# A routed mixture-of-experts layer: each row's expert choices renumbered by the block that serves them, half of them loaded during the last round, shared expert and routing tables interleaved anew

## The reference

```python
def moe_ffn(h, lp):
    x2 = h.reshape(bsz * t, d)
    scores = jax.nn.sigmoid((x2 @ lp['w_router']).astype(F32))          # 64 experts
    choice = scores + lp['b_router'].astype(F32)
    ...                                                                  # 4 of 8 expert groups
    _, idx = lax.top_k(jnp.where(expert_mask, choice, -jnp.inf), TOP_K)  # 8 choices of a row
    gate = jnp.take_along_axis(scores, idx, axis=1)
    gate = gate / jnp.sum(gate, axis=-1, keepdims=True) * ROUTE_SCALE
    routed = routed_experts(x2, idx, gate.astype(x2.dtype), lp['w_exp_gate'], lp['w_exp_up'], lp['w_exp_down'])
    shared = swiglu(x2, lp['w_sh_gate'], lp['w_sh_up'], lp['w_sh_down'])
    return (routed + shared).reshape(bsz, t, d)
# swiglu(x, wg, wu, wd) = (silu(x @ wg) * (x @ wu)) @ wd, inner width 256
# layer: x1 = x + g1 * mix(...);  y = x1 + g2 * moe_ffn(rms_norm(x1) * (1 + sc2) + sh2)
```

## Time and profile before

| | |
|---|---|
| median of 3 runs | 1614.6 us (1612.56 to 1618.46) |
| profiled execution | 1618.61 us, its span 1616.7 us |
| mean granted TensorE clock | 0.967 |
| TensorE, VectorE, ScalarE, POOL busy | 93%, 41%, 22%, 31% of the span |
| first weight transfer issued; first gate-up | 895.1 us; 935.1 us |
| last down product ends; last scatter issued | 1554.1 us; 1557.7 us |

### The profile page before, as it was taken

One profiled execution on the slowest core, in us unless ns is written; L12 is line 12 of the kernel. 1 busy time (PEld: TensorE's weight loads), 2 busy tenths in 40 slices (PEclk: granted clock), 3 DMA queues, 4 the chain that ended last, 5 costly groups with the idle time before them and its releaser, 6 DMA issues.

```text
span 1616.7 us, 21285 instructions
## 1 busy us (share of the span) xinstructions
PE 1510.2 (93%) x8196; PEld 819.0 (51%) x8196; DVE 655.4 (41%) x1119; ACT 357.6 (22%) x674; POOL 499.7 (31%) x545
## 2 busy tenths in 40 slices
PE   4999998999999979999999899999999998999977
PEld 3444455777688758888445533333333333333323
DVE  4799981232322566447466511111111111111147
ACT  3111133422533323331223111111111111111120
POOL 3121101211000014000000356665666665666510
PEclk9999999999999889999899989999999999999979
DMA  9787644778322657648111799999899899979668
GB/s 311 267 325 286 235 161 159 273 281 291 127 79 72 198 187 271 200 161 315 64 67 40 293 403 417 409 413 395 319 364 412 325 420 398 362 273 411 241 261 335
DMA packets 138630, 437.30 MB, mean 270 GB/s; under 512 B 31574, under 2 KB 59594, under 8 KB 103726
## 3 DMA queue, kind: packets, MB, share of 16 engines
q0 software_dynamic: 65088, 303.29, 48.6%
q1 hardware_dynamic: 68128, 122.39, 21.9%
q10 hardware_dynamic: 5344, 10.65, 1.7%
HBM read 507.52 MB, written 45.61 MB: 342 GB/s over the span
## 4 chain that ended last, share of the span: by engine, by line
PE 81%; DMA 8%; DVE 3%; issue 3%; ACT 2%; POOL 1%; another core or an unknown queue 1%; SPq 0%; POOLq 0%; ACTq 0%; DVEq 0%
PE bank L2440 18%; PE bank L2078 14%; PE bank L1989 12%; PE bank L2465 9%; PE bank L2309 4%; DMA arena<-in_w_exp_up_dram,arena 4%; PE bank L2297 4%; PE bank L2426 3%; PE bank L2111 2%; DMA arena<-expert_rows 2%; PE bank L2513 1%; DMA arena<-in_w_in_dram 1%; PE bank L2096 1%; POOL arena L721 1%; PE bank L2236 1%
## 5 line engine op out<-in xcount | busy, mean ns | idle before, releaser
L2440 PE MATMUL bank<-arena 128*64 128x512 f32 x1536 | 348.5, 605 | 10.7 <-DMA arena<-in_w_exp_up_dram,arena 6.2
L2078 PE MATMUL bank<-arena 128*128 128x260 f32 x1024 | 237.5, 387 | 0.0
L2440 PEld LDWEIGHTS bank<-arena 128*64 128x64 f32 x1536 | 108.3, 137 | 215.1 <-issue 209.4
L2078 PEld LDWEIGHTS bank<-arena 128*128 128x128 f32 x1024 | 191.9, 192 | 33.8 <-ACT arena L951 2.7
L1989 PE MATMUL bank<-arena 128*128 128x512 f32 (+1 forms) x448 | 189.8, 579 | 0.0
L2465 PE MATMUL bank<-arena 128*64 128x512 f32 x768 | 183.9, 603 | 5.5 <-issue 4.3
L1824 DVE TENSOR_TENSOR arena<-arena,bank 128x256 f32<-128x256 f32 x48 | 20.3, 423 | 362.0 <-ACT arena L1150 218.0
L1989 PEld LDWEIGHTS bank<-arena 128*128 128x128 f32 x448 | 83.5, 189 | 97.9 <-issue 90.5
L721 POOL DMA_INDIRECT arena<-in_w_exp_gate_dram,arena x96 | 96.0, 1000 | 72.7 <-issue 60.4
L721 POOL DMA_INDIRECT arena<-in_w_exp_down_dram,arena x96 | 96.2, 1002 | 29.8 <-issue 28.7
L721 POOL DMA_INDIRECT arena<-in_w_exp_up_dram,arena x96 | 96.1, 1001 | 29.3 <-issue 29.3
(11 more groups left out here) (454 smaller groups left out, 1790.6 us busy)
## 6 DMA issues: line engine op xcount, KB each, us to landing
arena<-in_w_ada_dram SPq DMA_DIRECT2D x24, 1024.0 KB, 7.6
arena<-in_w_merge_gate_dram SPq DMA_DIRECT2D x16, 1024.0 KB, 6.8
arena<-expert_rows SPq DMA_DIRECT2D x16, 1024.0 KB, 17.3
arena<-in_w_in_dram SPq DMA_DIRECT2D x6, 2048.0 KB, 13.7
gate_logits<-arena ACTq DMA_DIRECT2D x32, 260.0 KB, 6.0
arena<-gate_logits SPq DMA_DIRECT2D x8, 1040.0 KB, 6.3
arena<-in_cache_swa_k_dram SPq DMA_DIRECT2D x24, 192.0 KB, 5.9
arena<-in_cache_swa_v_dram SPq DMA_DIRECT2D x24, 192.0 KB, 3.4
```

The source lines that it names most:

```text
L2078: last = mm(o[:, 0:HALF], gate_place(q)[:, c, ms], hT[:, c, row_half[u % 2]], start=(c == 0), stop=(c == KC - 1))
L2440: ins = mm(bank[gu_bank[q]][r, :].rearrange("p (g n) -> p g n", g=2), xT[q][:, c, r], wgu[2 * q + lane][:, :, c, :], start=(c == 0), stop= ...
```

## The change

1. **Choices are numbered by block.** VectorE computes for each choice how many of the row's eight choices are served by an earlier block (`rank`), and the row code in the slot tables uses that rank. After the tables it permutes the gates in the same way. `yd` row 8 n + 0 is then the result that is written first.
2. **Bounds.** VectorE also takes the latest round of the choices of rank 1 and of rank 3 over all rows; two small TensorE products and a reduction bring both numbers to one partition (`bound_p`, `r_ready` 3). SP reads them.
3. **Early loads.** In the last round, SP loads slots 0 to 3 of all four tiles (8 loads of 1 MB) into buffers of weights that are done with, waiting for the scatters of the round that the bound names. Slots 4 to 7 stay behind the last scatter. VectorE takes slots 0, 1 and 7, TensorE slots 2 to 6, slots 2 and 3 ahead of the late ones. VectorE's sample operations move behind the last copy. Shared rows and x1 are loaded behind the first four early loads.
4. **Routing tables and shared expert.** The counts are split into a part without tile 3 and a part with it; the first tables are released ahead of the large multiply; TensorE's order is new, with `sh_gu` cut in two, down products of tiles 2 to 4 behind the slot tables, and other PSUM banks. POOL's first weight transfers go out by lane, in a new order.

The core of the diff (SP, POOL, VectorE, TensorE):

```diff
+            def early_load(t, h):
+                for q in range(3):
+                    sp.wait_ge(sem[f"yst{q}"], bound[h] * 16 + 16)
+                load(early[t][h], by_slot[t * P:t * P + P, 2 * h:2 * h + 2, :], pair_sem[t][h][0])
+            sp.wait_ge(sem["gu_done"], last * 3 + 1)
+            for h in range(2):
+                for t in range(2):
+                    early_load(t, h)
             sp.wait_ge(sem["gu_done"], last * 3 + 2)
+            load(shared_in, shared[0:SEQ, :].rearrange("(t p) d -> p t d", p=P), "bada_in")
...
+            sp.wait_ge(sem["dn_done"], last * 3 + 1)
+            for h in range(2):
+                early_load(3, h)
             sp.wait_ge(sem["gu_done"], last * 3 + 3)
+            for h in range(2):
+                early_load(2, h)
             for q in range(3):
                 sp.wait_ge(sem[f"yst{q}"], last * 16 + 16)
             load(s_rows, yd[SEQ * TOPK:TOK * TOPK, :], "x_in")
+            for t in range(NT):
+                for h in range(2):
+                    if h == 0:
+                        sp.wait_ge(sem["f_used"], 2 * t + 2)
+                    else:
+                        sp.wait_ge(sem["f_pe"], (1, 2, 3, 5)[t])
+                    load(late[t][h], by_slot[t * P:t * P + P, 2 * h + 4:2 * h + 6, :], pair_sem[t][h][0])
...
+            pool.wait_ge(sem["x1_out"], 16 * (TILES + 2))
+            load_gate_up(1, row[2], range(1))
             pool.wait_ge(sem["sh_gu"], TILES)
-            pool.wait_ge(sem["x1_out"], 16 * (TILES + 2))
-            load_gate_up(1, row[2])
+            load_gate_up(1, row[2], range(1, 2))
+            load_down(1, row[3], range(1))
             pool.wait_ge(sem["r_ready"], 2)
...
             for q in range(3):
                 block_gather(q, row[q])
+            load_down(2, row[4], range(1, 2))
+            pool.wait_ge(sem["sh_out0"], 32)
+            pool.wait_ge(sem["sh_out1"], 16)
+            load_gate_up(2, row[3], range(1))
             pool.wait_ge(sem["sh_y"], TILES)
-            load_down(1, row[3])
-            pool.wait_ge(sem["sh_out0"], 48)
-            pool.wait_ge(sem["sh_out1"], 32)
-            load_gate_up(2, row[3])
-            load_down(2, row[4])
+            load_down(1, row[3], range(1, 2))
+            load_gate_up(2, row[3], range(1, 2))
+            load_down(2, row[4], range(1))
...
+            step(stt(out=rank_key, in0=d_blk, scalar=float(TOPK), in1=slot_no..., op0=ALU.mult, op1=ALU.add))
+            step(tt_(r_cmp, rank_key.unsqueeze(3)..., rank_key.unsqueeze(2)..., ALU.is_gt))
+            step(dve.tensor_reduce(rank, r_cmp, AX, ALU.add))
+            step(tt_(row_code, row_code, rank, ALU.subtract))
...
-                if t in (0, 1, 3):
-                    sh_mid(t + 2 if t < 2 else 4)
+                if t == 3:
+                    sh_mid(3)
...
+            step(tt_(r_cmp, rank..., slot_no..., ALU.is_equal))
+            step(tt_(r_pick, r_cmp, gates..., ALU.mult))
+            step(dve.tensor_reduce(gates, r_pick, AX, ALU.add))
+            step(tt_(r_step, r_cmp[:, :, 1:4:2, :], d_in..., ALU.mult))
+            step(dve.tensor_reduce(r_late, r_step, AX, ALU.add))
+            dve.tensor_reduce(r_bound, r_late..., AX, ALU.min).then_inc(sem["r_tab_in"], 1)
...
+            positions_early()
+            positions_late()
+            sh_columns(0)
+            sh_gu(2, range(2))
+            sh_product(0)
             lane_items()
+            sh_columns(1)
+            sh_gu(2, range(2, KC))
+            sh_product(1)
+            sh_gu(3, range(4))
             slot_rows(0)
+            sh_gu(3, range(4, KC))
             slot_rows(1)
+            slot_rows(2)
             sh_gu(4)
             slot_rows(3)
             slot_rows(4)
+            sh_columns(2)
+            sh_columns(3)
...
+            sh_product(2)
+            sh_columns(4)
             pe.wait_ge(sem["r_ready"], 2)
+            sh_product(3)
+            sh_product(4)
...
+            for i in range(2):
+                ins = mm(bank[5][0:1, i * P:(i + 1) * P], r_bound[:, i:i + 1], ident, start=True, stop=True)
+            ins.then_inc(sem["r_tab"], 1)
+            gate_up(0, 1)
+            rows_transposed(0, 2)
+            pe.wait_ge(sem["r_ready"], 3)
+            down(0, 0)
+            middle_transposed(0, 1)
...
+            pe.wait_ge(sem["f_diag"], 1)
+            slots(0, (2, 3), early, 1)
             pe.wait_ge(sem["f_acc"], 1)
             pe.wait_ge(sem["y_v"], blocks)
...
+            slots(1, (2, 3), early, 2)
+            pe.wait_ge(sem["f_diag"], 4)
+            slots(2, (2, 3), early, 3)
...
+            slots(0, (4, 5, 6), late, 4)
+            pe.wait_ge(sem["f_acc"], 2)
+            slots(3, (2, 3), early, 5)
+            for t in range(1, NT):
+                slots(t, (4, 5, 6), late, 5 + t)
```

More of the change, by code:

```diff
@@ L1190, in _, with weights @@
                     block(p, q)
+            def weights(t, slots):
+                for k in slots:
+                    ins = fn(f_dg[:, t, k - 2, :], ident, ACT.Copy, scale=gates[:, t, k:k + 1])
+                ins.then_inc(sem["f_diag"], 1)
             for q in range(3):
                 block(last, q, front=q < 2)
+            for t in range(3):
+                weights(t, (2, 3))
             result_half(last, 2)
[L1196 to L1199 removed]
             act.wait_ge(sem["g_ps"], 4)
@@ L1856, in _ @@
             halves = [slice(c * 512, c * 512 + 512) for c in range(2)]
-            def base(t):
-                step(tt_(acc[t], acc[t], g2b, ALU.mult))
-                step(tt_(x1f[:, t, :], x1f[:, t, :], acc[t], ALU.add))
-            def choices(t):
-                for k in range(F_DVE):
-                    if k % 2 == 0:
-                        name, before = f_sem[t % 2][k // 2]
-                        dve.wait_ge(sem[name], before + 16 * (t // 2 + 1))
-                    y, g = fbuf[t % 2][k // 2][:, k % 2, :], gates[:, t, k:k + 1]
-                    if k == 0:
-                        ins = ts_(acc[t], y, g, None, ALU.mult)
-                    else:
-                        ins = stt(out=acc[t], in0=y, scalar=g, in1=acc[t], op0=ALU.mult, op1=ALU.add)
-                    ins.then_inc(sem["f_used"], 1)
-                    dve.wait_ge(sem["f_used"], F_DVE * t + k + 1)
@@ new lines, in rows_done @@
+            def rows_done(t):
+                name, before = pair_sem[t][1]
+                dve.wait_ge(sem[name], before + 32)
+                step(stt(out=acc[t], in0=late[t][1][:, 1, :], scalar=gates[:, t, 7:8], in1=acc[t], op0=ALU.mult, op1=ALU.add))
+                if t < NT - 1:
+                    dve.wait_ge(sem["f_pe"], (4, 6, 7)[t])
+                    for c in range(2):
+                        step(tt_(acc[t][:, halves[c]], acc[t][:, halves[c]], bank[F_BANK[t][c]][:, :], ALU.add))
+                    step(tt_(acc[t], acc[t], g2b, ALU.mult))
+                    tt_(x1f[:, t, :], x1f[:, t, :], acc[t], ALU.add).then_inc(sem["f_acc"], 1)
+                for c in range(2) if t == NT - 1 else ():
+                    dve.wait_ge(sem["f_pe"], 8 + c)
+                    step(tt_(acc[t][:, halves[c]], acc[t][:, halves[c]], bank[F_BANK[t][c]][:, :], ALU.add))
+                    step(tt_(acc[t][:, halves[c]], acc[t][:, halves[c]], g2b[:, halves[c]], ALU.mult))
@@ L2325, in routed, with sh_gu @@
                 router(i)
-            def sh_gu(t):
+            def sh_gu(t, part=range(KC)):
                 if t == 0:
@@ L2332, in sh_gu @@
                     pe.wait_ge(sem["sh_h"], t - 1)
-                for c in range(KC):
+                for c in part:
                     if t < NT:
@@ L2492, in _, with slots @@
             last.then_inc(sem["g_ps"], 1)
+            def slots(t, which, pairs, done):
+                for k in which:
+                    if k % 2 == 0:
+                        name, before = pair_sem[t][k // 2 % 2]
+                        pe.wait_ge(sem[name], before + (16 if k < 4 else 32))
+                    for c in range(2):
+                        ins = mm(bank[F_BANK[t][c]][:, :], f_dg[:, t, k - 2, :], pairs[t][k // 2 % 2][:, k % 2, c * 512:c * 512 + 512], start=(k == 2), stop=(k == 6))
+                        if k == which[-1] and (c == 1 or done == 8):
+                            ins.then_inc(sem["f_pe"], 1)
+            pe.wait_ge(sem["f_diag"], 1)
+            slots(0, (2, 3), early, 1)
             pe.wait_ge(sem["f_acc"], 1)
```

264 lines of the change are left out of this document (137 added, 127 removed).

## The result

The changed kernel takes 1595.05 us (median of 4 runs, 1593.83 to 1595.84), the kernel before 1614.8 in the same comparison (4 runs, 1612.56 to 1618.46): the ratio is 0.9879, 95% interval 0.9858 to 0.9901, faster by 1.2%. A second comparison on another chip gave 0.9881 (0.9859 to 0.9904). Forecast were 1590.7 us, range 1582 to 1602. The profiled execution took 1594.55 us with a span of 1592.7, 24.0 less than the span of before; the medians differ by 19.75 only, because the profiled execution of the kernel before was the longest of its runs.

A forecast was written before the change was run, and what follows sets the result against it. The end was taken as transfer-bound and the first third of the blocks as limited by weights. Gains of 17.4 us at the end and 6.5 us in the blocks, off the 1614.6 us median, gave 1590.7 us, range 1582 to 1602.

The forecast's parts named there:

- The end: Behind the last scatter: half the slot loads move ahead, TensorE then sets the end; gain 17.4 us, bounds 10 and 23.7.
- The skill's rule: Last scatter: engines alternate between queues packet by packet, so early loads lengthen it by 1.3 us, inside TensorE's 3 us.
- The blocks: Blocks up to 13: weights leave earlier and limit them, less new idle; gain 6.5 us, bounds 0 and 9.3.
- 7.1 us earlier: Routing: the first weight transfer, at 895.14 before, goes out 7.1 us earlier because the first tables are ready sooner.
- less about 0.5 us of new idle: Weight queue: eight transfers queued at once, the next waiting for the fifth shared gate-up, cost about 0.5 us.
- The first gate-up without pause: Block 0: gathers landed, TensorE unpaused, so the first gate-up takes 7.1 us, not 9.44, and ends 9.8 us earlier.
- The ranks, costed at nothing: VectorE's row-table chain: four new small operations of 0.23, 0.49, 0.45 and 0.2 us, none in the weights' chain.
- (b): Blocks give nothing, through new DMA idle or the saturated stretch taking the gain back: 1597.2 us; chance 0.18.
- (c): End limited by transfers or VectorE alone, TensorE's 36 us overlapping better: 1584.4 us; chance 0.10 at or below this.
- (d): Bound found on chip is the last round, so early loads queue behind the last scatter: 1616.6 us; chance 0.04.
- (e): Early loads starve the last weights by halving POOL's share, costing at most 5 us: 1595.7 us; chance 0.04.
- (f): TensorE's clock falls to the 1.2 GHz level at the end and stays, +36 us: 1626.8 us; chance 0.04.

The follow-up runs named there:

- Experiment 2: Changed kernel with only the early loads of slots 0 to 3 moved behind the last scatter, reloads of shared rows and x1 still early: 1597.01 us (0.9976).
- experiments 6 and 10: Changed kernel with slots 2 and 3 of tile 3 added by VectorE instead of TensorE, on two chips: 1574.06 us (0.9834) and 1597.79 us (0.9853).
- experiment 7: Changed kernel with tile 2's two early loads behind the last scatter, the other six ahead: 1608.0 us (0.9892).
- experiment 5: Changed kernel with block 0's gathers issued ahead of the three weight transfers on GpSimd's queue: 1583.32 us (0.9893).
- the front alone: Changed kernel's front, ranks included, with the end of the kernel before: 1594.99 us (0.9978).
- the second pair of traces: Kernel before and changed kernel, both unedited, traced again: the former takes 1621 to 1624 us on those chips, the latter 1604.36 us (0.9881).
- the three new fronts in the table: Changed kernel (1595.05 us), the same run again (1604.36 us), and its front with the end of the kernel before (1594.99 us).
- the changed kernel's second trace: The changed kernel run again without edits, as yardstick on another chip: 1604.36 us (0.9881).
- experiments 8 and 9: Kernel before with only ranks, bounds and gates in rank order added, run twice: 1628.11 us (1.0033), then 1626.44 us beside 1621.12.
- experiment 1: Changed kernel with early loads of slots 0 to 3, and the reloads queued behind them, waiting for the last round's scatters: 1611.59 us (1.0066).
- end 12.3 us: Changed kernel's end, with ranks and bounds, on the front of the kernel before: 1588.87 us (0.9923).
- the six kernels on the faster chips: The edited kernels of the first six experiments, run where the kernel before took 1599 us: 1611.59, 1597.01, 1594.99, 1588.87, 1583.32 and 1574.06 us.

## Why the prediction was right, step by step

Forecast were 23.9 us less, measured are 19.75 by the medians. That the two profiled executions differ by 24.0, the forecast almost to the point, is chance. The end gave 1.5 us less than forecast and the blocks some 3 less.

**The end, 17.4 us forecast, 15.9 measured (62.6 to 46.7; 46.4 again).** The mechanism is as forecast: half of the slot rows in the unused half of the last round (share 1.00 where 0.48 was), then TensorE for 84 instructions with one pause of 0.52 us. Experiment 2 shows that the early bytes are all of it (63.8 us without them), experiments 6 and 10 that TensorE is then the bound (3.4 us of instructions less, 3.2 to 3.7 us of end less). The 1.5 us of error are small terms: counted from the end of the last down product, TensorE's slot products were to end 38.1 us later (1592.2 less 1554.1) and end 39.8 later (1585.83 less 1546.0), 0.9 us of it in the first 24 products (11.3 us for 10.4), 0.6 around the sample rows with the wait of 0.52, 0.3 in the last 56 (24.31 for 24.0); VectorE's tail then follows 0.2 us closer. Whether the loads would get through was called "barely": tile 2's two are issued last, and the first of them left SyncE at 1538.00 and had landed at 1552.2 (the chain of waits has 14.18 us for it); VectorE stood 0.38 us for it, and TensorE came to the other without a pause.

**The skill's rule.** The Trainium skill (DMA: Bandwidth & Descriptors, "Queues, rings and completion order") has the engines take turns between queues that have work, from which I estimated 1.3 us more for the last scatter. The direction is right, the size is not: 7.9 us beside tile 2's two loads, 2.8 without early loads (experiment 2) and 2.9 without these two (experiment 7), 5 us more. The slack that I called 3 us covered it but for 0.52 us, because VectorE's and TensorE's work on early slots does not wait for the scatter. The first gathers, queued behind three weight transfers in their own queue, took 10.0 us and not 4.8; issued ahead of them they were there within 8 (experiment 5: issued at 917.47 into a queue that had run empty, transposes at 925.35 without a wait). I had no term for that.

**The blocks, 6.5 us forecast.** The first pair of traces says 8.1 (last down product 1554.08 to 1546.0), and that would have been read as a forecast slightly too low. The ratios say less: the front alone gains 0.22% (0.06 to 0.38), 3.5 us, and the second pair of traces has the last down product 1.3 us sooner (1552.44 to 1551.17). Two terms are now known. From the first score product to the first weight it is 93.3 us before and 86.9 after (801.48 to 888.35), 6.4 us less where I had 7.1. The new idle of the DMA engines is 1.5 us and not 0.5 (the mean of the three new fronts in the table is 5.0, of the two traces of before 3.5), from the hole at 913 to 918, in which GpSimd waits for the fifth shared gate-up, and some in the wait of 8.01 us for the store of shared rows. That leaves 6.4 - 1.5 = 4.9 us at block 13. The mis-sized terms are thus "7.1 us earlier", by 0.7, and "less about 0.5 us of new idle", by 1.0; the other 1.4 us down to 3.5 lie within the interval. The rule behind it, that the start of the weights and not that of TensorE decides up to block 13, fits every trace; but the sign that I named for it, a weight stall still there before block 13, is missing in both traces of the changed kernel.

**The first gate-up without pause, wrong.** I had the gathers landed when TensorE got to the transposes, no pause, and full clock. They landed 2 us after TensorE was there (925.96; a pause of 2.16 us), and the product took 10.05 us; in the window below the granted clock is 0.69 on average, between the levels of 2.4 and 1.2 GHz.

```profile
930.00:940.00 10.00, 9.88 (x32) 3.12 (x32) 0.00 (x0) 0.00 (x0) 6.93 (x7) 0.69 0.98 388
```

It seems to have cost nothing: the changed kernel's second trace (7.1 us) reached block 13 no sooner (207.1 us after its first weight, against 205.1).

**The ranks, costed at nothing.** I put four small operations (1.4 us) into the chain of the row tables and nothing into that of the weights. In the old order they cost 5 us (experiments 8 and 9). What is left of that price in the new order no run measured; its first step is there, as TensorE waits 2.26 us for VectorE's first slot matrices in the changed kernel, where it waited 0.57. Front with ranks 0.9978 and ranks alone 1.0033 make the new order, ranks in both, worth 0.55%, 8.8 us.

**The rivals.** (b), the blocks give nothing, is nearer to the truth than the first traces show, as 3.5 of 6.5 us came. (c) did not occur: TensorE, not the transfers, was the limit, though experiment 6 put the transfers next at once. (d) was tried as experiment 1: where I had a wash, 1616.6, it is 0.66% slower than before; I left out that TensorE's order makes 64 products follow the last early load. (e) was no loss to the weights in the last round: TensorE ran 36.48 of 37 us. (f) did not occur: the clock was 1.00 from 1514 to 1583.

**Left open.** The sum of parts (front 3.5 and end 12.3 us) is 3.6 us below the whole (19.4 us). Both parts pay for the ranks, and the whole pays once; the 5.4 us of that price would explain it within the intervals, but no run removed the ranks from the new front. And the blocks behind block 13 take 436 to 437 us in the six kernels on the faster chips and 452 to 464 on the others, whatever the kernel. I had expected 436 to 437 for the kernel before too when it ran again, and it took 454.8. The windows show it as DMA engines that are less busy and deliver less, and as pauses of TensorE (experiment 6, then the changed kernel again):

```profile
1120.00:1300.00 180.00, 180.00 (x860) 66.28 (x856) 26.02 (x43) 26.55 (x58) 121.62 (x134) 1.00 0.96 377
```

```profile
1120.00:1300.00 180.00, 171.81 (x790) 64.05 (x788) 24.70 (x42) 25.60 (x56) 110.81 (x123) 0.96 0.89 342
```

What holds them back there was not found.

## What to carry to other kernels

When a stage is bound by a saturated DMA stretch, cost an edit by what it does to the first transfer and to the holes in the queue that feeds it; when the matrix engine starts said nothing here. Work added to another engine can open such a hole two waits away (ranks on VectorE, shared products on TensorE, weights on GpSimd's queue). Where loads are moved ahead of a barrier, keep their order that of their use, and expect the transfer that the barrier waits for to take longer beside those issued last.

## What the runs showed of the hardware

- A scatter of GpSimd's queue (128 rows of 4 KB) took 2.7 to 3.3 us from issue to SyncE's next load without early loads or with the early ones issued 17 us before, and 6.9 to 7.9 with two loads of 1 MB issued some 10 us before on SyncE's queue. A gather took 4.8 us alone and 10.0 us with three weight transfers ahead of it in its own queue.
- Behind a pause of 2.30 us TensorE was granted 0.62 and 0.65 of its clock for 9.4 us, between its levels of 2.4 and 1.2 GHz, and 24 matmul instructions took 2.8 us longer than at 1.00 (experiment 9 against the second trace of before). Behind pauses of 0.57 and 0.63 us at the same place it fell to 0.68 in one trace of before and stayed at 1.00 in the other.
- The kernel before took 1599 us on two chips and 1615 to 1624 on the others, 1.5%; the traces have 16 to 28 us of difference in the blocks behind block 13, at 342 to 362 against 375 to 381 GB/s between 1120 and 1300 us.
- Between executions, stages that no edit touches moved the router's first product from 799 to 806 us. A single pair of traces can't tell a gain of 4 us in the front; the length between two marks inside it does (93.3 us in the five traces of the old order, 86.9 to 87.5 in the nine of the new).
